# Three row buffers and denser row requests in a PEER layer, and x passed in columns-first order as well

## The reference

```
q = xt @ w_pq                                   # 8 heads x 2 halves x 128
scores = q . sub_keys                           # 128 keys per half
expert_idx, gate = top 16 of the 16 x 16 sums   # per token and head, softmax over the 16
u = expert_u[idx];  act = gelu(u . x_token)     # 16384 experts of width 2048
out = sum(gate * act * expert_v[idx])
```

## Time and profile before

| | us |
|---|---|
| median of three runs | 1946.47 |
| the profiled execution | 1946.43 |
| its span, first to last instruction | 1944.3 |
| PE busy | 1834.1 (94%) |
| DVE busy | 1356.7 (70%) |
| POOL busy | 1022.5 (53%) |
| ACT busy | 1015.9 (52%) |

### The profile page before, as it was taken

The page is one execution under the profiler, slowest core; times in us unless marked ns, Lnnn a source line. Parts: engine busy times, 40 slices in busy tenths (PEclk is TensorE's granted clock), DMA queues, the critical chain, the costliest instruction groups (busy, mean ns, idle before and its releaser), DMA issues.

```text
span 1944.3 us, 30584 instructions
## 1 busy us (share of the span) xinstructions
PE 1834.1 (94%) x9326; PEld 1590.6 (82%) x9326; DVE 1356.7 (70%) x2047; ACT 1015.9 (52%) x1846; POOL 1022.5 (53%) x732
## 2 busy tenths in 40 slices
PE   9999999999999999988888888798999999999996
PEld 7888888888899998977777778697888888888885
DVE  4555676767656546656555556965899999888888
ACT  4455555544666665544444444455555555555553
POOL 0000231200789997888888886812565655344314
PEclk9999999999999999998888899999999999999998
DMA  7777775565656667988878788886999999999993
GB/s 227 241 244 233 232 233 175 189 212 169 199 176 209 209 208 234 240 240 220 239 221 238 213 245 265 267 287 221 341 389 372 386 381 354 392 380 379 371 343 97
DMA packets 198570, 508.92 MB, mean 262 GB/s; under 512 B 63312, under 2 KB 65552, under 8 KB 185264
## 3 DMA queue, kind: packets, MB, share of 16 engines
q1 hardware_dynamic: 131936, 392.09, 59.3%
q0 software_dynamic: 48144, 114.09, 18.8%
q10 hardware_dynamic: 18432, 2.11, 0.8%
HBM read 488.01 MB, written 18.97 MB: 261 GB/s over the span
## 4 chain that ended last, share of the span: by engine, by line
PE 65%; POOL 20%; issue 7%; DVE 5%; DMA 2%; ACT 1%; DVEq 0%; POOLq 0%; ACTq 0%; SPq 0%
POOL gate_dram L2011 15%; PE ps L521 14%; PE ps L523 14%; PE ps L522 14%; PE ps L768 6%; PE ps L808 6%; PE ps L809 6%; PE ps L774 4%; POOL u_rows L1998 2%; POOL split_lo L1976 2%; DVE split_lo L1534 2%; DMA u_rows<-in_expert_u,dot_rows 1%; DVE v_lo L1835 1%; DVE pick_n L1713 1%; PE ps L511 0%
## 5 line engine op out<-in xcount | busy, mean ns | idle before, releaser
L1078 ACT ACTIVATE split_hi<-raw 128x512 fp32r<-128x512 f32 x512 | 308.7, 625 | 359.8 <-PE ps L774 313.0
L768 PE MATMUL ps<-act_both,split_hi 128*128 128x448 f32 x2048 | 484.8, 381 | 0.0
L768 PEld LDWEIGHTS ps<-act_both,split_hi 128*128 128x128 f32 x2048 | 386.3, 199 | 27.8 <-ACT split_hi L1078 0.3
L1200 ACT ACTIVATE v_hi<-v_tile 128x1024 fp32r<-128x1024 f32 x248 | 263.3, 1063 | 255.8 <-PE ps L809 252.0
L774 PE MATMUL ps<-act_both,split_lo 128*128 128x224 f32 x2048 | 291.5, 285 | 81.7 <-DVE split_lo L1534 77.8
L774 PEld LDWEIGHTS ps<-act_both,split_lo 128*128 128x128 f32 x2048 | 281.3, 199 | 103.6 <-DVE split_lo L1534 89.3
L2011 POOL DMA_INDIRECT gate_dram<-pick_n,places x192 | 332.0, 1729 | 58.5 <-issue 58.5
L1776 DVE TENSOR_TENSOR v_lo<-v_tile,v_hi 128x1024 fp32r<-128x1024 f32 x248 | 303.1, 1247 | 62.0 <-ACT v_hi L1200 60.8
L1275 DVE TENSOR_TENSOR split_lo<-raw,split_hi 128x512 fp32r<-128x512 f32 x304 | 231.6, 768 | 162.8 <-ACT split_hi L865 161.9
L865 ACT ACTIVATE split_hi<-raw 128x512 fp32r<-128x512 f32 x344 | 216.4, 631 | 226.9 <-PE ps L523 224.4
L1534 DVE TENSOR_TENSOR split_lo<-raw,split_hi 128x512 fp32r<-128x512 f32 x368 | 274.6, 777 | 82.1 <-ACT split_hi L1078 69.8
(11 more groups left out here) (227 smaller groups left out, 2329.5 us busy)
## 6 DMA issues: line engine op xcount, KB each, us to landing
raw<-in_u_tiles SPq DMA_DIRECT2D x256, 512.0 KB
v_tile<-in_expert_v SPq DMA_DIRECT2D x256, 512.0 KB
raw<-in_w_in SPq DMA_DIRECT2D x112, 512.0 KB
raw<-in_w_out SPq DMA_DIRECT2D x32, 512.0 KB
raw<-in_w_pq SPq DMA_DIRECT2D x32, 512.0 KB
gate_dram<-zeros SPq DMA_DIRECT2D x24, 512.0 KB, 5.7
gates<-gate_dram POOLq DMA_DIRECT2D x64, 192.0 KB
gate_dram<-pick_n,places POOLq DMA_INDIRECT x192
```

The lines of the kernel that those rows point to most:

```text
L768: return nc.tensor.matmul(ps[:, bank, 0:2 * UT].rearrange("p (a t) -> p a t", a=2), split_hi[:, q % SPLITS, i * P:(i + 1) * P], act_both[: ...
L1078: nc.scalar.activation(split_hi[:, q % SPLITS, :], raw[:, q // 2, q % 2, :], ACT.Copy).then_inc(hi_ready, 1)
L1200: nc.scalar.activation(v_hi[:, unit % UNITS, :], v_tiles[unit % RING][:, :], ACT.Copy).then_inc(v_hi_ready, 1)
```

## The change

The diff, shortened:

```
-DOT_SLOTS, DOT_AT = 2, 22
+DOT_SLOTS, DOT_AT, DOT_EVERY, DOT_FROM = 3, 20, 4, 12
-PREFETCH = 55
+PREFETCH = 53
+        x_turned = at("x_turned", [KT, SEQ], f32, W0 + 73728)
-        x1_own = at("x1_own", [D], f32, W0 + 98304 + 8192)
-        u_slots = [at(f"u_rows{i}", [D], f32, W0 + 98304 + 16384 + 8192 * i) ...]
+        x1_own = at("x1_own", [D], f32, W0 + 98304)
+        u_slots = [at(f"u_rows{i}", [D], f32, W0 + 98304 + 8192 + 8192 * i) ...]
 SP, start:
-                sp.dma_start(x_piece(x_nat, n), x_piece(x..., n)).then_inc(x_in[n], 16)
+                sp.dma_start(x_turned[:, 4 * n:4 * n + 4, :], x_cols_first[:, 4 * n:4 * n + 4, :]).then_inc(x_in[n], 16)
             dense(w_in_v, 0, 0, False)
+            sp.dma_start(x_nat[:, :, :], x.rearrange("a (b p) d -> (a p) b d", p=P)).then_inc(x_nat_in, 16)
 SP, U stage:
-            with sp.Fori(1, DOT_AT - 1) as i:
-                u_pair(i)
-            sp.wait_ge(picked_in, 128); sp.wait_ge(topk_done, 2); sp.wait_ge(x1_out, X1_OUT)
-            for g in range(4):
-                sp.dma_start(x1_own[...], x1_dram[...]).then_inc(own_in, 16)
-            with sp.Fori(DOT_AT - 1, PREFETCH) as i:
+            with sp.Fori(1, PREFETCH) as i:
                 u_pair(i)
 PE, start:
-            keep_busy(14, 3)
-            for f in range(8): ... turn(F_X + f, ...); keep_busy((0, 8, 0, 5, 0, 5, 0, 18)[f], 3)
+            keep_busy(42, 3)
+            pe.sem_inc(turned, 8)
 ACT, start:
-            turned_hi(F_X)
-            for q in range(4):
-                split(0, q)
+            for f in range(8):
+                if f % 2 == 0:
+                    act.wait_ge(x_in[f // 2], 16)
+                nc.scalar.activation(act_hi[:, 2 * f:2 * f + 2, :], x_turned[:, 2 * f:2 * f + 2, :], ACT.Copy)...
+                if f % 2 == 1:
+                    split(0, f // 2)
 DVE, start: the same, with act_lo = x_turned - act_hi, and split(0, f // 2) behind each odd f
 DVE, residual:
+                dve.wait_ge(x_nat_in, 16)
 DVE, U stage:
-            dve.wait_ge(picked_in, 128)      # was ahead of pairs 18 to 21
             with dve.Fori(PAIRS_A // 2, DOT_AT // 2) as i: ... u_pair(i * 2 + s, s)
+            dve.wait_ge(picked_in, 128)
             dve.wait_ge(own_in, 64)
             (then one row per pair as before, slot j % 3 in place of j % 2)
 POOL:
-                        j = DOT_SLOTS + (n - 24) // 6
-                        return j if n >= 24 and n % 6 == 0 and j < DOTS else 0
+                        j = DOT_SLOTS + (n - DOT_FROM) // DOT_EVERY
+                        return j if n >= DOT_FROM and n % DOT_EVERY == 0 and j < DOTS else 0
-                    for j in range(DOT_SLOTS):
+                    pool.wait_ge(x1_out, X1_OUT)
+                    load_u_row(0)
+                    for g in range(4):
+                        eng.dma_start(x1_own[...], x1_dram[...]).then_inc(own_in, 16)
+                    for j in range(1, DOT_SLOTS):
                         load_u_row(j)
 POOL, behind the 32 applied gate pairs:
                     pool.wait_ge(v_free, 1)
+                    for bank in range(4):
+                        pool.wait_ge(act_out[bank], 16 + 8 * PAIRS)
                     for j in range(2):
                         load_row(j)
-                    for bank in range(4):
-                        pool.wait_ge(act_out[bank], 16 + 8 * PAIRS)
```

More of the change, by code:

```diff
@@ L105, in layer_kernel @@
 def layer_kernel(nc, x, w_in, sb_norm_w, ret_norm_w, w_out, ln1_w, ln1_b, w_pq, sub_keys,
-                 expert_u, expert_v, ln2_w, ln2_b, tables, small_tables, u_tiles, out):
+                 expert_u, expert_v, ln2_w, ln2_b, tables, small_tables, u_tiles, x_cols_first, out):
     f32, f32r, u32 = mybir.dt.float32, mybir.dt.float32r, mybir.dt.uint32
@@ L200, in layer_kernel @@
         places_u = at("places_u", [2, P], u32, T0 + 2048)
-        x1_own = at("x1_own", [D], f32, W0 + 98304 + 8192)
-        u_slots = [at(f"u_rows{i}", [D], f32, W0 + 98304 + 16384 + 8192 * i) for i in range(DOT_SLOTS)]
+        x1_own = at("x1_own", [D], f32, W0 + 98304)
+        u_slots = [at(f"u_rows{i}", [D], f32, W0 + 98304 + 8192 + 8192 * i) for i in range(DOT_SLOTS)]
         ps = ctx.enter_context(nc.psum_tensor("ps", [P, 8, COLS], f32))
@@ L893, in turned_hi @@
                                          ).then_inc(turn_hi, 1)
-            turned_hi(F_X)
-            for q in range(4):
-                split(0, q)
+            for f in range(8):
+                if f % 2 == 0:
+                    act.wait_ge(x_in[f // 2], 16)
+                nc.scalar.activation(act_hi[:, 2 * f:2 * f + 2, :], x_turned[:, 2 * f:2 * f + 2, :], ACT.Copy
+                                     ).then_inc(turn_hi, 1)
+                if f % 2 == 1:
+                    split(0, f // 2)
             def to_proj(stride, first):
@@ L1291, in turned_lo @@
                                       ).then_inc(turn_done, 1)
-            turned_lo(F_X, 0)
-            for q in range(4):
-                split(0, q)
+            for f in range(8):
+                dve.wait_ge(turn_hi, f + 1)
+                vec.tensor_tensor(act_lo[:, 2 * f:2 * f + 2, :], x_turned[:, 2 * f:2 * f + 2, :],
+                                  act_hi[:, 2 * f:2 * f + 2, :].bitcast(f32), ALU.subtract).then_inc(turn_done, 1)
+                if f % 2 == 1:
+                    split(0, f // 2)
             with dve.Fori(0, SB_AT) as i:
@@ L1632, in dot, with u_pair @@
                                          accum_out=dots[:, half, bass.ds(j, 1)]).then_inc(dot_used, 1)
-            def u_pair(pair, parity, j=None):
+            def u_pair(pair, parity, j=None, slot=None, landed=None):
                 for k in (2, 3):
@@ L1638, in u_pair @@
                     if j is not None and k == 2:
-                        dve.wait_ge(u_row_in[parity], pair * 8 - (DOT_AT + parity) * 8 + 16)
-                        dot(j, parity, 0)
+                        dve.wait_ge(u_row_in[slot], landed)
+                        dot(j, slot, 0)
                 add_halves(pair, 0, 2 * parity)
@@ L1644, in u_pair @@
                     if j is not None and k == 4:
-                        dot(j, parity, 1)
+                        dot(j, slot, 1)
             def softmax_start():
@@ L1751, in _ @@
                     u_pair(i * 2 + s, s)
+            dve.wait_ge(picked_in, 128)
             dve.wait_ge(own_in, 64)
-            with dve.Fori(DOT_AT // 2, (DOT_AT + DOTS) // 2) as i:
-                for s in range(2):
-                    u_pair(i * 2 + s, s, i * 2 + (s - DOT_AT))
+            with dve.Fori(0, DOTS // 6) as i:
+                for n in range(6):
+                    u_pair(i * 6 + (DOT_AT + n), n % 2, i * 6 + n, n % DOT_SLOTS, i * 32 + (16 * (n // DOT_SLOTS) + 16))
+            for j in range(DOTS // 6 * 6, DOTS):
+                u_pair(DOT_AT + j, j % 2, j, j % DOT_SLOTS, 16 * (j // DOT_SLOTS) + 16)
             dve.wait_ge(dot_used, 2 * DOTS)
@@ L2041, in _ @@
                             scatter(h, b)
-                    for j in range(DOT_SLOTS + (PH * sum(per_head) - 24) // 6, DOTS):
+                    for j in range(DOT_SLOTS + (PH * sum(per_head) - DOT_FROM) // DOT_EVERY, DOTS):
                         load_u_row(j)
@@ L2157, in columns_first, with x_columns @@
     return np.ascontiguousarray(tiles.transpose(0, 1, 3, 5, 4, 2)).reshape(PAIRS * RAWS * P, 2 * COLS)
+def x_columns(a):
+    return np.ascontiguousarray(a.reshape(SEQ, KT, P).transpose(2, 1, 0))
 _INS = ["x", "w_in", "sb_norm_w", "ret_norm_w", "w_out", "ln1_w", "ln1_b", "w_pq", "sub_keys",
@@ L2171 @@
     named = [(n, np.ascontiguousarray(inputs[n])) for n in _INS] + [("tables", cst), ("small_tables", small),
-                                                                     ("u_tiles", columns_first(np.asarray(inputs["expert_u"])))]
+                                                                     ("u_tiles", columns_first(np.asarray(inputs["expert_u"]))),
+                                                                     ("x_cols_first", x_columns(np.asarray(inputs["x"])))]
     for name, a in named:
```

8 lines of the change are left out of this document (2 added, 6 removed).

## The result

The changed kernel takes 1882.48 us (median of 4 runs, 1877.92 to 1893.67); the kernel before, run beside it, 1944.94 (4 runs, 1941.05 to 1950.26). The ratio is 0.9686, with a 95% interval of 0.9635 to 0.9736. The forecast was 1891, with a range of 1870 to 1922, and faster at 0.92. The profiled execution of the changed kernel took 1877.92 us with a span of 1876.1, so 68.5 us less than the profiled 1946.43 of before. All that follows is read from this execution unless another is named.

A forecast was written before the change was run, and what follows sets the result against it. POOL's own instructions were taken to set the dot stage's pace and the end. 1946.43 (profiled execution) - 57.7 (earlier first row sum) + 2.6 (clock after PE's halt) = 1891 us; range 1870 to 1922.

The forecast's parts named there:

- The pace T: Dot stage: time from one row request to the next, 10.4 us, between 9.9 and 10.8; before, 13.9.
- POOL's start and the tail of scatters: POOL's scatters: row 3 at 786, then 28 periods, 1.8 and 67 scatters of 1.99 us, ending at 1212.3.
- The gates: POOL's 32 gate pairs after the scatters: 63.4 us plus 5 (0 to 13) for running beside V splits.
- The dots' move: POOL, after the gates: row requests 3.3, side results and dots 22 (19 to 24), weights 0.9 us; first row sum 1317.
- The reserve: POOL's 67.6 us wait for the V stage: the most to be had if its scatters don't get shorter.
- The U stage's end: End of the U stage at 1231 us, 106 earlier than 1337, including some 4 for splits under gates.
- The halt: V stage: PE runs dry by 1269 and waits some 45 us for POOL.
- The start: PE's first product at 18.9 us instead of 17.55, perhaps at the lower clock; +2 us, range -1.3 to +7.
- The clock after the halt: V stage after PE's long halt: lower granted clock, 2.6 us paid once more.
- Rival 1: POOL does not decide the end and the U stage's 106 us stay whole: 1842 us, 3 in 100.
- Rival 2: The queues set the dot stage's pace at 11 to 12.3 us: 1908 to 1944 us, 15 in 100.
- Rival 3 and 4: Rows or u_tiles late, POOL waits at `dot_used`: 1964 at T=13, 5 in 100; period stays 13.9: 1989, below 1 in 100.

The follow-up runs named there:

- two buffers: The changed kernel with two row buffers instead of three, requests still every 4 scatters: 1885.40 us, ratio 0.9727.
- the dots moved first: The changed kernel with 8 instead of 32 gate pairs ahead, dots moved before the side results, one row request before the wait for stores: 1835.43 us, ratio 0.9446.
- 8 pairs ahead: The changed kernel with 8 instead of 32 gate pairs applied ahead of the row and side-result requests: 1844.57 us, ratio 0.9501.
- the start alone: The kernel before with only the new start (x passed by columns as well, no PE transposes of it): 1942.94 us, ratio 1.0017.
- 40 pairs ahead: The changed kernel with 40 instead of 32 gate pairs applied ahead: 1899.65 us, ratio 0.9775.
- the start kept warm: The changed kernel with 104 instead of 42 idle transposes at the start: 1886.25 us, one run.
- the two other spacings: The changed kernel with row requests every six scatters from scatter 24 (1959.01 us), or every five from scatter 12 (1885.92 us), instead of every four.

## Why the prediction was right, point by point

The mechanism was the forecast one: POOL's chain took over from the dot stage, with one long halt of PE in the V stage. The time is 8.5 us below the forecast in the medians, 13.4 in the profiled executions (1891.3 against 1877.92), of which 11.9 lie ahead of the first row sum and 1.5 behind it. By the prediction's own steps:

- **The pace T: right, mis-sized by 0.3.** Forecast 10.4, measured 10.09. The bounds of 9.9 and 10.8 held. Within them both terms were off: a scatter cost (204.5 + 32.9)/108 = 2.20 us, near the dear end of 2.24, and a request 996 ns and the gap, 1.30 and not 1.79. Four and one are 10.1.
- **POOL's start and the tail of scatters: right.** Row 3 was asked for at 787.24 (forecast 788 with the 2 us of the start), row 31 at 1069.85 (1079.2: 28 times the 0.3 of T), the last scatter ended at 1209.9 (1214.3). The tail gave back part of it: from row 31's request to the last scatter's end it was 140.0 us and not 135.1, a scatter at 2.07 and not 1.99. "Scatters end at 1200.9" misreads the trace of before: the last scatter ended at 1195.66, and two row requests stood behind it until 1200.87. The sum doesn't suffer, since it takes the 8.0 us to the first gates from 1200.87 on; measured are 6.9 from the last scatter's end.
- **The gates: right.** 68.5 us from 1216.76 to 1285.23; forecast 63.4 + 5. The strict reading of the Trainium skill (SBUF — State Buffer, "Who interferes with whom"), in which the two engines exclude each other by a lock, was worked out to an estimate of up to 74 us. It would have needed DVE's splits all along, and DVE had stopped by 1250.3. Beside splits a pair does take longer (1.53 for a product that alone takes 1.00, near 1220), so the two do disturb each other.
- **The dots' move: mis-sized, and outside its bounds.** Forecast 3.3 for two row requests, 22 (19 to 24) from the first side result to the dots, and 0.9, 26.2 in all; measured 1305.07 - 1285.23 = 19.8. The 22 was 16.3 (1287.82 to 1304.14), below even the lower bound of 19: with DVE idle a row request took 1.0 and a side result 0.95 us. This is 6.4 of the 12 us by which the first row sum came earlier than forecast (1305.07, not 1317); 4.4 are the scatters, 1.1 the reading of the gates.
- **The reserve: a bound that was passed.** "... the 67.6 us are the most that can be had from it" did not hold: the first row sum came 69.6 us earlier and the time fell by 68.5. That the numbers are so close is in part luck. The gates were done 13.0 us later than before and the stretch behind them was 15.0 us shorter, and neither has to do with the wait of 67.6.
- **The U stage's end: too late by 17 us, and of no account.** Forecast 1231, measured 1214.0; 9.9 are T, 4 the splits under gates, which never met since U was over at the first gate; the other 3 are not accounted for. From this comes a wait that I did not forecast: PE stood still for 7.3 us before its first V product at 1221.32. ACT's high part of the first gated activations waited 7.5 us for POOL's gate product and DVE's low part 7.6 us for ACT's. "The V stage can begin, since the first gates are applied by 1222" fails by its order: the gates were what PE waited for. It is in no sum, since POOL's chain ended later anyway.
- **The halt: right.** "Some 45 us" from 1269; measured 51.1 from 1256.5. It is longer because U ended earlier, and because DVE was ready for the first row sum 29.0 us into the V stage and not 37.7 (of which, before, 3.2 were waiting for the dots); it ends earlier because POOL does.
- **The start: the place right, the size on the safe side.** First product at 17.25 and not 18.9: the first split had its data by 10.75 (forecast 12.5). At the lower clock, as one of the two cases had it. By the start of the U stage the changed kernel is 1.6 us behind (558.3 against 556.7), close to the 2 of the forecast. By the other reading of the Trainium skill (TensorE: Matmul & The Clock Gate, "Part 4: PE-mode transpose"), that transposes don't count as activity, the kernel kept busy with 104 of them would also have begun at 0.43 us a product; it began at 0.23. The earlier trace rows had said so.
- **The clock after the halt:** 2.6 forecast; the stretch from the first row sum to the end grew by 1.1.
- **The rivals.** Rival 1 (POOL doesn't decide) would have given 1842; the halt, the two runs with other gates ahead and the run with a request after every five scatters refute it. Rival 2: the share went to 1.03 as feared, at 317 GB/s, and PE waited for no tile: the share is no bound here. Rival 3 and 4 would have shown as waits at `dot_used` and a pace of 13.9; neither is in the trace.

One thing stays open in the pace. 10.09 us is also exactly PE's own, though POOL waits for nobody: its idle times are all "issue". With four scatters after the dots POOL would need 4 x 2.04 + 1.30 = 9.5 us, and the scatter just ahead of each request is the longest, 2.44. Of the four scatters between two requests the two that run beside a half of a dot are the long ones (824.87 beside the dot at 824.66, 818.82 beside the one at 819.32); the other two take 1.55. So POOL may be stretched until it fits DVE's rhythm, which follows PE's. With two buffers, where the fit is lost at times, single periods of 9.4 us occur. That speaks for it, but no run tried it.

## What to carry to other kernels

A stage that is made shorter by 123 us gave 68, because another engine's fixed chain ended later than the stage: before cutting a wait, follow the chain of every other engine up to the next place where they meet, and read the smaller reserve there (67.6 us on POOL's row) as a first estimate of what there is to win, before the steps of that chain themselves change (here by +13.0 and -15.0 us). What stands in that chain and isn't needed at the meeting point (24 pairs of gates, a side result ahead of the dots) costs nothing as long as it is covered and nearly its full length once the cover is gone (43.1 us for 24 pairs of 1.90); moving it behind gave another 2.5% here (0.9686 to 0.9446, on two chips). Where one edit carries several things, time each alone: here the spacing made the gain, the third buffer and the new start nothing that could be told from noise. Dots from pair 20 on, the earlier `PREFETCH`, the moved waits and the loads of `x1_own` on POOL's queue were not taken out one by one.

## What the runs showed of the chip that I had not expected

- **POOL's indirect DMA instructions take longer beside DVE.** A scatter's shortest is 1.55 us; beside dots it takes up to 2.46, and once, near the first dot, 2.57. A side result takes 0.95 with DVE idle; beside DVE's V splits it takes twice as long, as here in the version with the dots moved first. DVE's splits there run from 1249.22 to 1250.45, from 1251.48 to 1252.71 and from 1253.75 to 1254.98, so the first of these three rows lies between two splits, and the others run beside one:

```profile
1250.45 0.95 POOL L2078 DMA_INDIRECT picked_act<-act_dram,picked  x1 [0.30 <-issue]
1251.71 1.82 POOL L2078 DMA_INDIRECT picked_act<-act_dram,picked  x1 [0.30 <-issue]
1253.84 1.97 POOL L2078 DMA_INDIRECT picked_act<-act_dram,picked  x1 [0.30 <-issue]
```

  The fixed order of work thus has prices that hang on what DVE does: the same eight fetches took 10.1 us in the changed kernel's halt and 15.3 with 8 pairs ahead, partly beside DVE's splits.
- **A wait of some 6.5 us comes and goes.** PE waits for ACT (L758, `split_hi`) near 670 us in some executions (6.7 us with 8 pairs ahead and with the start alone, 6.5 with the dots first, with 40 pairs ahead and with the start kept warm) and not in others (none there in those of before, of the changed kernel, of the two other spacings and of two buffers). The code of that stretch is the same in all. With it, the first gate product lies anywhere from 1216.8 to 1231.9 us in kernels that are the same up to there. The cause is open, and no run tried it; two profiles of such kernels are better compared from a common point on, as in the table above, than by their totals.
- **A DMA share of 1.03 held nobody up** at 317 GB/s, where the earlier trace rows have one of 0.99 at 384.
